# One more attention job of the output projection from split parts, with fewer constant products and moved subtractions

## The chip, the cores and the metric

The kernel runs on one core of a Trainium2 chip. The metric is the device time of one execution in microseconds (us). The kernel before takes 1575.31 us, the median of 3 runs (1574.83 to 1578.89).

## The reference, cut to what matters

The program computes two decoder layers over 256 positions of width 2048. What the change touches lies in the first layer's mixer and in the second layer's:

```python
def even_layer(x, ...):                      # layer 0
    proj = rms_norm(x, norm_w) @ w_in        # q, k, v, indexer parts, GLU input
    attn = dsa_attention(...)                # 8 heads x 128 = 1024 channels
    conv = conformer_conv(glu_in, ...)       # GLU -> causal depthwise conv, 31 taps,
                                             # 1024 channels -> LayerNorm over channels -> silu
    return x + jnp.concatenate([attn, conv], axis=-1) @ w_out

def odd_layer(x, norm_w, pool_w, pool_scale):  # layer 1
    # d = windowed mean of rms_norm(x) minus itself, 4 groups of 512 channels
    mixed = jnp.einsum('bsgc,gce->bsge', d, pool_w)
    return x + pool_scale * mixed
# each layer is followed by a mixture of experts (hier_moe)
```

LayerNorm needs the mean and the variance over the 1024 channels, so the convolution must be complete before either is known, and nothing of `conv @ w_out` can begin before the variance.

## The kernel before, in words

All 256 positions stand on chip. Weights come in blocks of 1 MB (128 partitions x 2048 numbers) into a ring of 8 slots. A block is used in one of two ways.

*Split stream.* Each half block (a unit, 128 x 1024) is rounded by ScalarE into `split_hi` (line 688, type fp32r), then VectorE writes the rest, block minus high part, into `split_lo` (line 1092). TensorE makes three products of each pair of tiles, high x high, high x low and low x high (`product`, lines 1785 to 1787). There are SPLITS = 4 buffers of each: ScalarE may write unit u only when TensorE has used unit u-4 (`mixer_used`). `split_past(name, n)` on ScalarE or VectorE means: have all units up to n past the end of job `name` in the stream.

*Direct.* `direct_job` (line 1866) multiplies the fp32 block as it lies in the ring by fp32 data. No splitting is done for it. Each such product shows as two records on TensorE.

The output projection of layer 0 has 8 jobs: `wa0` to `wa3` (attention half of the input, output columns by 512) and `wc0` to `wc3` (convolution half). Before, `wa0`, `wa1`, `wa2` are direct and `wa3` and all `wc` come from the stream. A streamed job has 4 units of 12 products (`out_job`), and a function `beside_...(q)` puts other work ahead of its unit q. The order on TensorE is written out by hand: `wa0`, `wa1`, `wa2`, `wa3`, `wc0` to `wc3`. Beside `wa2` stand the two halves of the channel sum for the mean (`channel_sum`, line 1933, the second half waits for all 248 steps of the convolution); beside `wa3` the sums of squares for the variance (`squares_sum`, line 1944, ahead of unit 0) and the spreading of the row scales (`rstd`, line 2019, ahead of unit 2).

The convolution is done on VectorE, one instruction for each tap and chunk (`convolve(n)`: the next n of 248 instructions, line 1137), in order with everything else that VectorE does. Around the change VectorE's order is: 20 and 31 taps, the low part of the attention output (`attn_parts[1]`, line 1092), the addition of `wa0` to x (`add_job`, line 1329), the remaining taps, two units of `wa3`, scaling of the mean (1343), subtraction of it (1347), two units of `wa3`, addition of `wa1`, variance (1351), diagonal of row scales (1354), addition of `wa2`, two units of `wc0`, then `scale_conv(j)` (1362), `silu(j)` (1368) and `lo_of_conv(j)` (1092), which alternate with ScalarE (870, 874, 688). `wc0` waits for `lo_of_conv(0)`.

At the very start TensorE multiplies a tile of ones (`keep_busy_small(24)`, 8 and 8, line 1736) between transpositions of x, whose results nobody reads.

In the second layer's mixer, `pool_split(u)` (VectorE part at line 1096) writes the low part of unit u of the pooling weights, scaled by the norm weights. VectorE's order there is: last additions of the experts, `sum_squares(2)` (1088), scaling of the band matrices (1697), then 8 low parts of the pooled input `dT` with `pool_split` 1, 2 and 3 behind the first, third and fifth. TensorE's first product waits for the eighth low part and for units 0 and 1.

SyncE issues the weight loads in ring order and waits for a slot to be free: for a direct block until TensorE used it, for a streamed block until VectorE wrote its low part.

Of the kernel before, what the change touches and what calls it, by code (L numbers as in the profile page):

```python
# [102 lines left out]


STREAM = [(name, 8) for name in ("ag0", "ag1", "kvi", "iq0", "iq1", "q0", "q1", "ag2", "ag3")]
STREAM += [(name, 4) for name in ("wa3", "wc0", "wc1", "wc2", "wc3")]
DIRECT = [f"wa{n}" for n in range(3)]

STREAM_END = {name: sum(k for _, k in STREAM[:i + 1]) for i, (name, _) in enumerate(STREAM)}

# [1 line left out]
def job_number(name):  # L112

    return sum(n not in STREAM_END and n not in DIRECT for n, _ in JOBS[:JOB_AT[name] + 1])

# [15 lines left out]
def build(nc, a):  # L131
    x_in, out = a["x"], a["out"]
    ctx = ExitStack()
    with ctx:
# [102 lines left out]
        def cat_cut(at, a, b):  # L237

            return [cat[:, at + i * a * b:at + (i + 1) * a * b].rearrange("p (a b) -> p a b", b=b) for i in range(2)]
# [3 lines left out]
        attnT = xn[:, NT * HEADS * HD:].rearrange("p (h s) -> p h s", h=HEADS)  # L243
        attn_parts = cat_cut(2 * D, HEADS, SEQ)
# [224 lines left out]

        DIRECT_BLOCKS = range(DIRECT0, DIRECT0 + 2 * len(DIRECT))  # L470

# [36 lines left out]
        def wait_for_job(eng, name):  # L508

            if name in STREAM_END:  # L510
                eng.wait_ge(mixer_used, STREAM_END[name])
            elif name in DIRECT:
                eng.wait_ge(direct_used, 2 * DIRECT.index(name) + 2)
            else:
# [171 lines left out]
        def _(act):  # L686
# [35 lines left out]
            def split_past(name, more):  # L722

                split_to(STREAM_END[name] + more)
# [130 lines left out]
            copy(attn_parts[0], attnT).then_inc(attn_hi, 1)  # L855
            split_past("ag3", 4)
            for h in range(2):
                act.wait_ge(ln_step, 2 + h)
                half = slice(4 * h, 4 * h + 4)
                nc.scalar.activation(vsq[:, half, :], conv[:, half, :], ACT.Square).then_inc(squared, 1)  # L860
# [209 lines left out]
        def _(dve):  # L1070
# [14 lines left out]
            def sum_squares(i):  # L1085

                dve.wait_ge(sq_done, 8 * (i + 1))
                nc.vector.tensor_reduce(sumsq[:, i, :], part_sq[:, i], X, ALU.add).then_inc(sum_done, 1)
# [15 lines left out]
            def wait_job(name):  # L1104
                wait_for_job(dve, name)
# [20 lines left out]
            def convolve(more):  # L1126

                end = min(at[1] + more, taps_open[0])
                for n in range(at[1], end):
                    c, w = conv_ops[n]  # L1130
                    tap = cw_sb[:, w * CC + c:w * CC + c + 1]
                    if w == 0:
                        ts(conv[:, c, :], uT[:, c, 0:SEQ], tap, vec_sb[:, V_CB + c:V_CB + c + 1], ALU.mult, ALU.add) \
                            .then_inc(conv_step, 1)
                    else:
                        dve.wait_ge(conv_step, n - 1)
                        stt(out=conv[:, c, :], in0=uT[:, c, w:w + SEQ], scalar=tap, in1=conv[:, c, :],  # L1137
                            op0=ALU.mult, op1=ALU.add).then_inc(conv_step, 1)
                at[1] = end

            def split_to(end, taps=0):

                for u in range(at[0], end):
                    b, n = split_block(u), 2 * (KVW + IKW) if u // 2 in kvi_at else HALF
                    dve.wait_ge(mixer_hi, u + 1)
                    low(split_lo[:, u % SPLITS, 0:n], raw_half(b % RING, u % 2, n), split_hi[:, u % SPLITS, 0:n]) \
                        .then_inc(mixer_lo, 1)
                    convolve(taps)
                at[0] = end

            def split_past(name, more, taps=0):
                split_to(STREAM_END[name] + more, taps)
# [75 lines left out]
            n = 0  # L1228
# [18 lines left out]
            n = 0  # L1247
# [83 lines left out]
            def add_job(name):  # L1331
                wait_job(name)
                for t, bank in enumerate(BANKS[name]):
                    add_x(int(name[-1]), t, bank)

            convolve(31)
            dve.wait_ge(attn_hi, 1)
            low(attn_parts[1], attnT, attn_parts[0]).then_inc(attn_lo, 1)
            add_job("wa0")
            convolve(CONV_TAPS)  # L1340
            split_past("ag3", 2)
            wait_job("mean")
            ts(mean_sb, ps[:, BANKS["mean"][0], 0:SEQ], 1.0 / CCH, None, ALU.mult).then_inc(ln_step, 1)
            dve.wait_ge(ln_step, 1)
            for h in range(2):
                half = conv[:, 4 * h:4 * h + 4, :]
                tt(half, half, mean_sb.unsqueeze(1).to_broadcast([P, 4, SEQ]), ALU.subtract).then_inc(ln_step, 1)
            split_past("ag3", 4)
            add_job("wa1")
            wait_job("var")  # L1350
            ts(rvar, ps[:, BANKS["var"][0], 0:NT], 1.0 / CCH, EPS, ALU.mult, ALU.add).then_inc(ln_step, 1)
# [330 lines left out]
            def pool_split(u):  # L1682
                dve.wait_ge(pool_hi, u + 1)
                for k in range(2):
                    cols = slice(k * 512, (k + 1) * 512)
                    last = low_of(split_lo[:, u % SPLITS, cols], raw_half((POOL0 + u // 2) % RING, u % 2)[:, cols],
                                  vec_sb[:, V_PN + 2 * u + k:V_PN + 2 * u + k + 1], split_hi[:, u % SPLITS, cols])
                last.then_inc(pool_lo, 1)

            moe_dve(0)  # L1690

            sum_squares(2)
            dve.wait_ge(band_in, 16)
            dve.wait_ge(rstd_done, 3)
# [3 lines left out]
            for i in range(8):  # L1698
                dve.wait_ge(pooled_hi, i + 1)
                low(dT[1][:, 2 * i:2 * i + 2, :], ps[:, i, :].rearrange("p (c s) -> p c s", c=2), dT[0][:, 2 * i:2 * i + 2, :]) \  # L1700
                    .then_inc(dT_out, 1)
                if i in (0, 2, 4):
                    pool_split(1 + i // 2)
            for i in range(8):
                g, t = i // 2, i % 2
                if i == 0:
# [20 lines left out]
        def _(pe):  # L1727
# [5 lines left out]
            def keep_busy_small(n):  # L1733

                for i in range(n):
                    mm(ps[:, 0, 0:P], ones[:], ones[:], start=True, stop=True)  # L1736

            pe.wait_ge(set_up, 1)
            keep_busy_small(24)
            pe.wait_ge(ident_in, 16)  # L1740

            def turn_vectors():
# [100 lines left out]
            def out_job(name, parts, between=lambda q: None):  # L1843

                start_job(name)
                for q in range(4):
                    between(q)
                    w = next_unit(2, 512)
                    for k in range(2):
                        for t, b in enumerate(BANKS[name]):  # L1850
                            last = product(ps[:, b, :], pick_parts(parts, ALL, 2 * q + k, slice(t * P, (t + 1) * P)),
                                           pick_parts(w, ALL, k), q == 0 and k == 0, q == 3 and k == 1)
                    last.then_inc(mixer_used, 1)

            def direct_job(name, src, between=lambda q: None):

                start_job(name)
                for q in range(4):
                    between(q)
                    b = DIRECT0 + 2 * int(name[-1]) + q // 2  # L1860
                    if q % 2 == 0:
                        pe.wait_ge(mixer_in[b % RING], mixer_landed(b))
                    w = raw_half(b % RING, q % 2).rearrange("p (k n) -> p k n", k=2)
                    for k in range(2):
                        for t, bank in enumerate(BANKS[name]):
                            last = mm(ps[:, bank, :], src[:, 2 * q + k, t * P:(t + 1) * P], w[:, k, :],  # L1866
                                      start=q == 0 and k == 0, stop=q == 3 and k == 1)
                    if q % 2:
                        last.then_inc(direct_used, 1)
# [132 lines left out]
            def beside_wa2(q):  # L2002
                if q == 0:
                    pe.wait_ge(conv_step, CONV_TAPS // 2)
                    channel_sum("mean", conv, 0)
                if q == 2:
                    pe.wait_ge(conv_step, CONV_TAPS)
                    channel_sum("mean", conv, 1)

            def beside_wa3(q):  # L2010
                if q == 0:
                    for h in range(2):
                        pe.wait_ge(squared, h + 1)
                        squares_sum(h)
                if q == 2:
                    start_job("rstd")
                    pe.wait_ge(diag_done, NT)
                    for t in range(NT):
                        last = mm(ps[:, BANKS["rstd"][0], t * P:(t + 1) * P], ones[:], rstd_diag[:, t, :], start=True, stop=True)
                    last.then_inc(job_done, 1)  # L2020
# [3 lines left out]
            for j in range(4):  # L2024
                turn_first(j)
                if j % 2:
                    keep_busy_small(8)
            channels_job("ag0", beside_ag0)
            channels_job("ag1", beside_ag1)
            pe.wait_ge(row_scale_out, 1)  # L2030
# [11 lines left out]
            pe.wait_ge(oT_out, 4)  # L2042
            direct_job("wa0", attnT)
            direct_job("wa1", attnT)
            direct_job("wa2", attnT, beside_wa2)
            pe.wait_ge(attn_lo, 1)
            out_job("wa3", attn_parts, beside_wa3)

            def beside_wc(n, q):
# [217 lines left out]
```

## Time and profile before

| | |
|---|---|
| profiled execution | 1575.78 us, of which the span of instructions is 1573.9 us |
| TensorE (PE) busy | 1539.9 us, 98% |
| VectorE (DVE) busy | 1393.9 us, 89% |
| ScalarE (ACT) busy | 1082.8 us, 69% |
| chain that ended last | PE 86%, DVE 11%, ACT 2% |
| DMA | 471.62 MB, mean 300 GB/s |

TensorE is nearly always busy, so the table alone does not tell what bounds a stage. The slices of the page show the first mixer (to about 380 us) as the place where TensorE and VectorE are both near full while DMA falls to 84 to 177 GB/s; the two expert stages run TensorE full with DMA at 340 to 380 GB/s. The chain gives VectorE a share of 11%, nearly all of it in the first mixer.

### The profile page before, as it was taken

How to read it: one execution, taken by the hardware profiler on the slowest of the kernel's cores; microseconds unless marked ns; L12 is line 12 of the kernel's file. 1: busy time of each engine (PE TensorE's matmuls, PEld its weight loads, DVE VectorE, ACT ScalarE, POOL GpSimd, SP SyncE). 2: the span in 40 equal slices, each digit the busy share in tenths (PEclk: the TensorE clock that was granted, in tenths of full speed). 3: DMA queues.
4: the chain of work that ended last, by engine and by line, in shares of the span. 5: the costliest groups of instructions: out<-in, count | busy, mean ns of one | idle time of the engine just before them, and what ended most of it. 6: DMA issues, size and time to landing. Idle time of an engine off the chain costs nothing.

```text
span 1573.9 us, 21864 instructions
## 1 busy us (share of the span) xinstructions
PE 1539.9 (98%) x7520; PEld 1269.2 (81%) x7520; DVE 1393.9 (89%) x1698; ACT 1082.8 (69%) x1287; POOL 12.8 (1%) x23
## 2 busy tenths in 40 slices
PE   9999999999999999999999999999999999999998
PEld 8998795677788878878887877778888887888886
DVE  4898989766999999999999987699999999999997
ACT  5444352164878777877877785587877887787785
POOL 0000100000000000000000000000000000000000
PEclk9999999999999999999999999999999999999999
DMA  8974442543999999999999993299999999999993
GB/s 230 362 249 140 151 144 84 177 154 122 342 370 377 362 362 370 368 345 375 382 350 359 376 359 105 83 339 386 375 348 379 376 362 345 370 375 349 369 371 142
DMA packets 159756, 471.62 MB, mean 300 GB/s; under 512 B 20922, under 2 KB 40844, under 8 KB 159284
## 3 DMA queue, kind: packets, MB, share of 16 engines
q1 hardware_dynamic: 158148, 466.85, 80.8%
q10 hardware_dynamic: 1520, 3.63, 0.6%
q8 instruction: 51, 0.84, 0.2%
q14 instruction: 37, 0.30, 0.0%
HBM read 468.34 MB, written 4.21 MB: 300 GB/s over the span
## 4 chain that ended last, share of the span: by engine, by line
PE 86%; DVE 11%; ACT 2%; issue 1%; POOL 0%; DVEq 0%
PE ps L1785 26%; PE ps L1787 26%; PE ps L1786 26%; DVE work L1137 3%; DVE split_lo L1092 3%; PE ps L1731 2%; PE ps L2104 2%; PE ps L2090 1%; PE ps L1766 1%; DVE cat L1092 1%; PE ps L1736 1%; ACT split_hi L688 1%; PE ps L1886 0%; PE ps L1866 0%; DVE work L1258 0%
## 5 line engine op out<-in xcount | busy, mean ns | idle before, releaser
L688 ACT ACTIVATE split_hi<-ring 128x1024 fp32r<-128x1024 f32 x860 | 904.6, 1058 | 298.2 <-PE ps L1787 286.1
L1092 DVE TENSOR_TENSOR split_lo<-ring,split_hi 128x1024 fp32r<-128x1024 f32 x860 | 1026.4, 1218 | 93.0 <-ACT split_hi L688 58.3
L1785 PE MATMUL ps<-split_hi,cat 128*128 128x512 f32 (+1 forms) x1744 | 687.1, 394 | 11.7 <-DVE split_lo L1092 5.4
L1787 PE MATMUL ps<-split_hi,cat 128*128 128x512 f32 (+1 forms) x1744 | 677.8, 389 | 0.0
L1786 PE MATMUL ps<-split_lo,cat 128*128 128x512 f32 (+1 forms) x1744 | 677.5, 388 | 0.0
L1785 PEld LDWEIGHTS ps<-split_hi,cat 128*128 128x128 f32 x1744 | 328.2, 188 | 93.8 <-issue 15.6
L1787 PEld LDWEIGHTS ps<-split_hi,cat 128*128 128x128 f32 x1744 | 327.6, 188 | 68.5
L1786 PEld LDWEIGHTS ps<-split_lo,cat 128*128 128x128 f32 x1744 | 328.1, 188 | 63.6
L1785 PE MATMUL ps<-cat,split_hi 128*128 128x256 f32 x384 | 111.5, 290 | 7.4 <-DVE split_lo L1092 7.4
L1787 PE MATMUL ps<-cat,split_lo 128*128 128x256 f32 x384 | 110.1, 287 | 0.0
L1786 PE MATMUL ps<-cat,split_hi 128*128 128x256 f32 x384 | 110.0, 287 | 0.0
L1137 DVE SCALAR_TENSOR_TENSOR work<-work,cw_sb 128x256 f32<-128x256 f32 x240 | 99.4, 475 | 0.0
L1785 PEld LDWEIGHTS ps<-cat,split_hi 128*128 128x128 f32 x384 | 75.1, 196 | 9.4 <-DVE split_lo L1092 4.7
L1787 PEld LDWEIGHTS ps<-cat,split_lo 128*128 128x128 f32 x384 | 75.1, 196 | 0.0
L1786 PEld LDWEIGHTS ps<-cat,split_hi 128*128 128x128 f32 x384 | 75.0, 195 | 0.1
L1092 DVE TENSOR_TENSOR cat<-ps,cat 128x512 fp32r<-128x512 f32 (+1 forms) x56 | 46.4, 835 | 2.1 <-ACT cat L688 1.9
L688 ACT ACTIVATE cat<-ps 128x512 fp32r<-128x512 f32 (+1 forms) x56 | 38.9, 706 | 10.0 <-PE ps L2199 6.0
L1565 DVE TENSOR_TENSOR x_sb<-ps,x_sb 128x1024 f32<-128x1024 f32 x32 | 38.8, 1216 | 4.8 <-PE ps L2104 4.8
L1866 PE MATMUL ps<-ring,xn 128*128 128x512 f32 x96 | 41.8, 593 | 0.7 <-ACT xn L688 0.7
L2104 PE MATMUL ps<-cat,pickT 128*128 128x512 f32 x128 | 33.8, 391 | 3.1 <-DVE cat L1092 3.1
L1866 PEld LDWEIGHTS ps<-ring,xn 128*128 128x128 f32 x96 | 18.2, 190 | 23.1 <-issue 21.5
L2104 PEld LDWEIGHTS ps<-cat,pickT 128*128 128x128 f32 x128 | 23.9, 188 | 8.8 <-DVE cat L1092 3.9
(200 smaller groups left out, 686.3 us busy)
## 6 DMA issues: line engine op xcount, KB each, us to landing
ring<-in_w_gate SPq DMA_DIRECT2D x128, 1024.0 KB, 6.1
ring<-in_w_up SPq DMA_DIRECT2D x128, 1024.0 KB, 6.3
ring<-in_w_down SPq DMA_DIRECT2D x128, 1024.0 KB, 6.1
ring<-in_w_in_e SPq DMA_DIRECT2D x16, 1024.0 KB, 7.1
ring<-in_w_out_e SPq DMA_DIRECT2D x16, 1024.0 KB, 5.1
ring<-in_w_in_e SPq DMA_DIRECT2D x30, 512.0 KB, 4.6
ring<-in_pool_w_o SPq DMA_DIRECT2D x4, 1024.0 KB, 5.7
ring<-in_w_in_e SPq DMA_DIRECT2D x12, 256.0 KB, 6.1
```

The source lines that it names most:

```text
L688: return nc.scalar.activation(out, in_, ACT.Copy, scale=scale)
L1092: return tt(dst, full, hi.bitcast(F32), ALU.subtract)
L1137: stt(out=conv[:, c, :], in0=uT[:, c, w:w + SEQ], scalar=tap, in1=conv[:, c, :], op0=ALU.mult, op1=ALU.add).then_inc(conv_step, 1)
L1565: tt(cols, ps[:, bank:bank + 2, :].rearrange("p b n -> p (b n)"), cols, ALU.add).then_inc(m["x_moved"], 1)
L1731: return nc.tensor.transpose(dst, src, ident[0:n, 0:n])
L1736: mm(ps[:, 0, 0:P], ones[:], ones[:], start=True, stop=True)
L1766: last = mm(ps[0:20, LOGIT_BANKS[l][0], 0:SEQ], router_w[:, l, c, :], hT32[:, c, :], start=c == 0, stop=c == KC - 1)
L1785: mm(out, sh, mh, start=start, stop=False, **how)
L1786: mm(out, sh, ml, start=False, stop=False, **how)
L1787: return mm(out, sl, mh, start=False, stop=stop, **how)
L1866: last = mm(ps[:, bank, :], src[:, 2 * q + k, t * P:(t + 1) * P], w[:, k, :], start=q == 0 and k == 0, stop=q == 3 and k == 1)
L2104: last = mm(ps[:, bank, :], pickT[:, t, :], y[part][:, b * 512:(b + 1) * 512], start=part == 0, stop=part == 1)
```

## The change

`wa2` leaves the direct jobs and joins the stream ahead of `wa3`; the channel sums, sums of squares and row scales move from `wa2`/`wa3` to later places; VectorE takes the four units of `wa2` and one unit of `wa3` between convolution steps and adds `wa0` ahead of the attention's low part; the products of ones fall from 24 to 17 and from 8 to 3 twice; `pool_split(1)` moves ahead of `sum_squares(2)`, and units 2 and 3 behind the first and fourth low part.

```diff
-STREAM += [(name, 4) for name in ("wa3", "wc0", "wc1", "wc2", "wc3")]
-DIRECT = [f"wa{n}" for n in range(3)]
+STREAM += [(name, 4) for name in ("wa2", "wa3", "wc0", "wc1", "wc2", "wc3")]
+DIRECT = [f"wa{n}" for n in range(2)]
...
@@ ScalarE
             split_past("ag3", 4)
             for h in range(2):
+                split_past("ag3", 6 + h)
                 act.wait_ge(ln_step, 2 + h)
...
@@ VectorE
             convolve(31)
+            add_job("wa0")
             dve.wait_ge(attn_hi, 1)
             low(attn_parts[1], attnT, attn_parts[0]).then_inc(attn_lo, 1)
-            add_job("wa0")
+            split_past("ag3", 4)
+            convolve(20)
+            split_past("wa2", 1)
             convolve(CONV_TAPS)
-            split_past("ag3", 2)
             wait_job("mean")
...
-            split_past("ag3", 4)
+            split_past("wa2", 4)
             add_job("wa1")
...
+            pool_split(1)
             sum_squares(2)
...
-                if i in (0, 2, 4):
-                    pool_split(1 + i // 2)
+                if i in (0, 3):
+                    pool_split(2 + i // 3)
...
@@ TensorE
-            keep_busy_small(24)
+            keep_busy_small(17)
...
                 if q == 0:
                     pe.wait_ge(conv_step, CONV_TAPS // 2)
                     channel_sum("mean", conv, 0)
-                if q == 2:
+            def beside_wa3(q):
+                if q == 0:
                     pe.wait_ge(conv_step, CONV_TAPS)
                     channel_sum("mean", conv, 1)
-
-            def beside_wa3(q):
-                if q == 0:
+                if q == 2:
                     for h in range(2):
                         pe.wait_ge(squared, h + 1)
                         squares_sum(h)
-                if q == 2:
+                if q == 3:
                     start_job("rstd")
...
                 if j % 2:
-                    keep_busy_small(8)
+                    keep_busy_small(3)
...
             direct_job("wa1", attnT)
-            direct_job("wa2", attnT, beside_wa2)
             pe.wait_ge(attn_lo, 1)
+            out_job("wa2", attn_parts, beside_wa2)
             out_job("wa3", attn_parts, beside_wa3)
```

## Rows read from the trace of the kernel before

**Rows 1.** Timeline of VectorE, 269 to 312 us: start, length, instructions, idle before.
```profile
269.86 19.47 DVE L1137 SCALAR_TENSOR_TENSOR work<-work,cw_sb 128x256 f32<-128x256 f32 x49
289.25 2.35 DVE L1092 TENSOR_TENSOR split_lo<-ring,split_hi 128x1024 fp32r<-128x1024 f32 x2
291.52 0.41 DVE L1343 TENSOR_SCALAR work<-ps 128x256 f32<-128x256 f32 x1
291.97 2.36 DVE L1347 TENSOR_TENSOR work<-work 128x1024 f32<-128x1024 f32 x2
...
301.75 0.16 DVE L1351 TENSOR_SCALAR work<-ps 128x2 f32<-128x2 f32 x1 [3.95 <-PE ps L1944]
302.72 0.48 DVE L1354 TENSOR_SCALAR work<-const_sb,work 128x128 f32<-128x128 f32 x2 [0.81 <-POOL work L678]
303.12 1.28 DVE L1329 TENSOR_TENSOR x_sb<-ps,x_sb 128x512 f32<-128x512 f32 x2
...
310.00 1.23 DVE L1092 TENSOR_TENSOR split_lo<-ring,split_hi 128x1024 fp32r<-128x1024 f32 x1 [1.44 <-ACT split_hi L688]
311.15 1.28 DVE L1362 TENSOR_TENSOR work<-work,ps 128x512 f32<-128x512 f32 x2
```

**Rows 2.** Timeline of TensorE, 252 to 317 us.
```profile
252.47 27.73 PE L1866 MATMUL ps<-ring,xn 128*128 128x512 f32 x64 [0.69 <-ACT xn L688]
280.04 1.89 PE L1933 MATMUL ps<-work,ones 128*128 128x256 f32 x8
281.76 7.03 PE L1866 MATMUL ps<-ring,xn 128*128 128x512 f32 x16
289.39 1.99 PE L1933 MATMUL ps<-work,ones 128*128 128x256 f32 x8 [0.59 <-DVE work L1137]
...
298.08 3.63 PE L1944 MATMUL ps<-ones,work 128*128 128x1 f32 x32
...
305.98 0.39 PE L1785 MATMUL ps<-split_hi,cat 128*128 128x512 f32 x1
...
308.71 0.61 PE L2019 MATMUL ps<-work,ones 128*128 128x128 f32 x4
...
316.85 0.47 PE L1785 MATMUL ps<-split_hi,cat 128*128 128x512 f32 x1 [2.07 <-DVE cat L1092]
```

**Rows 3.** Timeline of ScalarE, one unit of the stream.
```profile
308.91 1.06 ACT L688 ACTIVATE split_hi<-ring 128x1024 fp32r<-128x1024 f32 x1 [1.61 <-PE ps L1787]
```

**Rows 4.** Stretches: PE, PEld, DVE, ACT, POOL busy, then granted clock, DMA.
```profile
301.60:305.30 3.70, 3.70 (x12) 2.89 (x12) 1.84 (x5) 0.00 (x0) 0.69 (x1) 0.56 1.05 402
...
314.80:316.85 2.05, 0.00 (x0) 0.03 (x1) 1.69 (x4) 2.05 (x4) 0.00 (x0) 1.00 0.28 114
```

**Rows 5.** Stretches, TensorE alone: busy, granted clock, DMA share, GB/s.
```profile
179.80:182.00 2.20, 0.18 (x1) 1.00 0.19 62
...
183.00:186.00 3.00, 3.00 (x16) 0.50 0.28 55
...
959.40:962.40 3.00, 0.00 (x1) 1.00 0.31 66
```

**Rows 6.** Timeline of the start on TensorE: products of ones, then unit 2.
```profile
1.08 7.52 PE L1736 MATMUL ps<-ones 128*128 128x128 f32 x48 [1.08 <-DVE ones L1076]
...
9.62 1.95 PE L1736 MATMUL ps<-ones 128*128 128x128 f32 x16
...
20.61 0.36 PE L1785 MATMUL ps<-cat,split_hi 128*128 128x256 f32 x1
```

**Rows 7.** Timeline of ScalarE at the start: unit 2 of the stream.
```profile
17.83 1.06 ACT L688 ACTIVATE split_hi<-ring 128x1024 fp32r<-128x1024 f32 x1 [4.19 <-DMA ring<-in_w_in_e]
```

**Rows 8.** Timeline of VectorE in the second mixer.
```profile
949.34 0.16 DVE L1088 TENSOR_REDUCE sumsq<-part_sq 128x2 f32<-128x8 f32 x1 [1.49 <-ACT xn L698]
...
954.12 1.41 DVE L1096 SCALAR_TENSOR_TENSOR split_lo<-ring,vec_sb,split_hi 128x512 fp32r<-128x512 f32 x2
...
960.48 1.88 DVE L1092 TENSOR_TENSOR cat<-ps,cat 128x512 fp32r<-128x512 f32 x3
```

## The prediction

> **What bounds the kernel now.** The page was read first, for the shares: TensorE is busy 98% of the span, which says little, since a busy TensorE in the first mixer can be one that merely fills the time until VectorE is ready. So the next view was the timeline of VectorE and TensorE side by side over the output projection. The reader should see two things. VectorE runs without a gap up to the last tap at 289.25 us [rows 1], and TensorE waits for exactly that tap: its second channel sum begins at 289.39 after 0.59 us of idle time put down to VectorE's line 1137 [rows 2]. So up to that point VectorE sets the time, TensorE is nearly level with it, and any work added to VectorE ahead of the last tap comes out in full. Behind the tap the bound changes: VectorE idles 3.95 us for the sums of squares [rows 1], TensorE is full until 314.8, and then idles 2.07 us for the low part of the first convolution chunk, which starts `wc0` at 316.85 [rows 2, 4]. From `wc0` on TensorE carries the chain (the additions, transpositions and expert stages follow it), so the start of `wc0` is what the change in this stage must be judged by. The expert stages are untouched; I take it that a shift arrives at the end in full, since TensorE waits there for no load.
>
> **The output projection, step by step.** A direct job is 32 records; 64 of them take 27.57 us (252.47 to 280.04), so one job is 13.8 us. Three-part products follow each other by 0.2275 us (12 between 305.98 and 308.71, one unit, 2.73 us), so a streamed job is 10.9 us [rows 2]. TensorE loses 2.9 us of work. In exchange VectorE gets four more subtractions and ScalarE four more copies.
>
> VectorE, ahead of the last tap. The attention's low part and the addition of `wa0` swap places; `wa0` is done at about 266.4, when VectorE comes, so both still end at 269.86. Then:
> - four units of `wa2`: a pair takes 2.27 us until the next starts (289.25 to 291.52), so 4.54 us, to 274.40. Their copies on ScalarE were made long before, in an idle stretch.
> - 20 taps at 0.396 us (49 between 269.86 and 289.25) [rows 1]: 7.91 us, to 282.31.
> - one unit of `wa3`. Its copy needs the buffer of `wa2`'s unit 0, which TensorE frees only when it has finished `wa1` (280.04), the first channel sum (to 281.76) and the 12 products (to 284.49) [rows 2], and drained them (0.2 us: the last product of the unit before 308.71 frees ScalarE at 308.91) [rows 3]. The copy lets VectorE start 1.09 us later (308.91 to 310.00) [rows 1, 3]: 285.78. **VectorE stands still for 3.5 us with the taps queued behind this wait**, and all of the LayerNorm behind the taps. This is the step that decides.
> - the subtraction, 1.14 us, and 29 taps, 11.48 us: the last tap ends at 298.40, against 289.25. That is 9.15 us later, of which 4.5 are the new units, 1.1 the advanced one and 3.5 the wait.
>
> TensorE meanwhile finishes `wa2` at 281.76 + 10.92 = 292.7 and has nothing until 298.4, since the second channel sum now stands ahead of `wa3`: 5.7 us idle.
>
> Behind the last tap, first at the full clock. Second channel sum from 298.54, and VectorE reads the mean at 300.6 (289.39 to 291.38 is 1.99, plus 0.1); scaling and both subtractions as in [rows 1], to 303.36. Then unit 1 of `wa3` to 304.5; TensorE did unit 0 by 303.0, waits, and does unit 1 to 307.3. The squares of ScalarE are ready by 305.4, so the sums of squares run 307.3 to 310.8 (3.49 us, the length it had) [rows 2]. From the start of those sums VectorE reads the variance 3.67 us later, the diagonals end 1.37 us after that (301.75 to 303.12) [rows 1]: 312.3. Next on VectorE stand the addition of `wa2` (1.2 us) and two units of `wc0` (2.3 us; before, the second of them was waited for until 310.00 anyway): 315.8. The row scales are spread by then even if TensorE's unit 2 runs at half rate. The first `scale_conv` starts at 315.8 against 311.15, and `wc0` 5.70 us later as before (311.15 to 316.85) [rows 1, 2]: 321.5. **So this stage costs +4.6 us with no clock lost.** TensorE's 2.9 us come back only as shorter waits. The bounds are +1.2 (if the 3.5 us wait should not be, by an earlier release that I don't see) and +8 with all clock losses below.
>
> **The clock.** After 2.0 us of idle time (180.0 to 182.0) TensorE worked at a granted clock of 0.50, that is 1.2 GHz, from 183 to 186 [rows 5]; after the tiny one-column sums of squares it had 0.56 over 301.6 to 305.3 [rows 4]. After 2.05 us of idle time from 314.8 and 3.0 us from 959.4 it kept 1.00 [rows 4, 5]. So a gap of two or three us may or may not do it; 5.7 us is far longer than the gap that did. I take it that the second channel sum runs at half rate: 1.7 us more, all of it on the chain, as VectorE, ScalarE and the sums of squares wait for it. `wa3` unit 0 behind it has 1.5 us of room. Bounds 0 and +2.7 (that unit too). TensorE then ends `wa3` at about 320 and waits some 3 us for `wc0` where it waited 2.07: `wc0` may start at 1.2 GHz too. Its second and third unit waited for VectorE before, which absorbs about half: between 0 and +0.8, with 0.5 taken.
>
> The Trainium skill (TensorE: Matmul & The Clock Gate, "Why this matters for your kernels") warns against idle gaps between bursts of matmuls, because the clock falls back to half rate after one. It speaks against this change at the 5.7 us gap: by it the stage costs +6.3, by the rows of 314.8 and 962.4 taken alone +4.6. The trace so far sides with it for the gap at 180 and not for the other two.
>
> **The start.** 17 instead of 24 products of ones remove 14 records at about 0.112 us (16 in 1.8) [rows 6], 1.6 us, since those removed are full-rate ones at the end; twice 10 records more remove 2.2 us. The first unit would begin 3 us earlier, at 11.0, ready data or not: the first x and gains are landed, and the first subtraction is done at about 10.9. But unit 2 needs a block whose copy starts at 17.83, held by DMA [rows 7]; its low part is ready 1.09 + 1.15 later, at 20.1, and its products begin at 20.61 today [rows 6]. So of 3.8 us removed 0.45 arrive, and TensorE idles 2.4 us ahead of unit 2. If that gap takes the clock down, unit 2 costs 1.7 more: bounds -0.45 and +1.25, and -0.4 taken, since gaps of 2.05 and 3.0 us left the clock up in [rows 4, 5]. Behind it TensorE is full to 100 us.
>
> **The second mixer.** VectorE is the chain from 953.5 to 962.36: eight low parts of 0.6 and three `pool_split` of 1.32 (954.12 to 955.44), the last low part ending where TensorE starts [rows 8]. `pool_split(1)` moves to 947.8, into the 1.49 us that VectorE idles before `sum_squares` at 949.34; 1.32 us fit, and its high part is done at 941. The eighth pooled tile is copied at 960.04, so the eighth low part can end at 961.0: **-1.3 us**. Bounds -1.5 and 0 (if `sum_squares` is pushed by as much). The new order of units 2 and 3 leaves them done by 958.6, ahead of group 1's need.
>
> SyncE's queue: the slots of `wa2` are now freed by its low parts, 14 us earlier, those of `wa3` a few us later. The blocks behind them (`wc2`, `wc3`) are used after 340, so nothing waits.
>
> **Sum**, against the profiled execution of 1575.78 (span 1573.9 plus 1.9 around it): +4.6 +1.7 +0.5 -0.4 -1.3 = +5.1, which gives 1580.9; that execution lies 0.5 above the median of 1575.31, so the forecast for a median is 1580.4, put at 1580.5. What a measurement of this kernel can tell from no change is 0.3%, 4.7 us: the forecast lies just beyond it.
>
> **Rivals.**
> - *The same chain, clock kept.* +4.6 -0.4 -1.3 = +2.9: 1578.3. For it: the two gaps without a fall. Against: neither was much over 3 us, and this one is 5.7.
> - *TensorE is the bound throughout.* Then the 2.9 us of the shorter job arrive, with 1.3 and 0.4: -4.6, 1570.7. It decides if VectorE's taps have slack of 9 us against TensorE. Against it stands the 0.59 us wait at 289.39 in [rows 2]: they have none. This is the case on the other side.
> - *No wait ahead of the advanced unit.* The stage costs +1.2, and the total is -0.5: 1574.8. For it: only that ScalarE is idle there. Against: the buffer is TensorE's to free.
> - *Clock lost at the start and at `wc0` in full.* +5.1 +1.7 +0.5: 1582.6.
>
> **How the numbers follow.** Forecast 0.55, clock kept 0.20, no wait 0.09, all clocks lost 0.08, TensorE bound 0.08. The forecast's own spread is 1578.5 to 1582.5, and about 0.39 of its 0.55 lies over +0.3%. Slower: 0.39 + 0.08 = 0.47. Faster: 0.06 of the TensorE case. Same: the rest, 0.16 + 0.20 + 0.09 + 0.02 = 0.47. The range leaves out the TensorE case and most of the case without a wait: 1576 to 1583.5.
>
> **What would show it.** The last tap near 298 instead of 289, with VectorE idle 3 us or more ahead of one subtraction, released by ScalarE's copy; TensorE idle over 5 us ahead of its second channel sum, and a granted clock near 0.5 there; `wc0` starting 6 us later; the second mixer's first product 1.3 us earlier relative to `sum_squares`; the start's unit 2 held by DMA at 17.8. I am wrong if VectorE does not idle ahead of that unit, or if TensorE waits for the taps by less than 2 us.

## The result, and the profile after

The changed kernel takes 1582.96 us, the median of 9 runs (1580.93 to 1585.17), against 1577.47 us for the kernel before (9 runs in all). The ratio is 1.0036, with a 95% interval of 1.0028 to 1.0045: slower by about 5.7 us. The forecast was +5.1 us, and 1580.5 us for the median. The profiled execution took 1582.92 us with a span of 1581.0, so 7.1 us more span than the one before. Single executions spread by several us, for a reason shown further down, so the account below is made of stretches of the traces, and what is faster or slower is told by the ratios.

The timeline of VectorE over the output projection, after (start, length, instructions, idle before), answers to [rows 1]:

```profile
269.27 4.62 DVE L1093 TENSOR_TENSOR split_lo<-ring,split_hi 128x1024 fp32r<-128x1024 f32 x4
273.82 8.00 DVE L1138 SCALAR_TENSOR_TENSOR work<-work,cw_sb 128x256 f32<-128x256 f32 x20
285.26 1.23 DVE L1093 TENSOR_TENSOR split_lo<-ring,split_hi 128x1024 fp32r<-128x1024 f32 x1 [3.45 <-ACT split_hi L688]
286.40 11.57 DVE L1138 SCALAR_TENSOR_TENSOR work<-work,cw_sb 128x256 f32<-128x256 f32 x29
301.92 0.42 DVE L1346 TENSOR_SCALAR work<-ps 128x256 f32<-128x256 f32 x1 [3.94 <-PE ps L1937]
...
312.45 0.16 DVE L1354 TENSOR_SCALAR work<-ps 128x2 f32<-128x2 f32 x1 [2.45 <-PE ps L1948]
...
315.02 2.35 DVE L1093 TENSOR_TENSOR split_lo<-ring,split_hi 128x1024 fp32r<-128x1024 f32 x2
317.34 1.29 DVE L1365 TENSOR_TENSOR work<-work,ps 128x512 f32<-128x512 f32 x2
```

The reader should see the third line: one subtraction of 1.2 us, preceded by 3.45 us of standing still, with 29 taps behind it. The last tap ends near 298, 9 us later than in [rows 1]. ScalarE's copy, for which it waited, could begin when TensorE had freed the buffer, and not before. The timeline of ScalarE:

```profile
284.17 1.06 ACT L688 ACTIVATE split_hi<-ring 128x1024 fp32r<-128x1024 f32 x1 [26.66 <-PE ps L1791]
```

ScalarE was idle for 26.66 us ahead of it, so it is a matter of the buffer and not of a busy engine. The timeline of TensorE, which answers to [rows 2]:

```profile
251.83 27.73 PE L1870 MATMUL ps<-ring,xn 128*128 128x512 f32 x64 [0.69 <-ACT xn L688]
279.40 1.89 PE L1937 MATMUL ps<-work,ones 128*128 128x256 f32 x8
...
298.12 3.75 PE L1937 MATMUL ps<-work,ones 128*128 128x256 f32 x8 [5.89 <-DVE work L1138]
...
308.78 3.63 PE L1948 MATMUL ps<-ones,work 128*128 128x1 f32 x32
...
323.05 0.73 PE L1789 MATMUL ps<-split_hi,cat 128*128 128x512 f32 x1 [3.01 <-DVE cat L1093]
```

The second channel sum waits 5.89 us for the last tap and then takes 3.75 us where it took 1.99. The stretches of TensorE (busy, granted clock, DMA share, GB/s) say why, and answer to [rows 5]:

```profile
292.30:298.10 5.80, 0.00 (x0) 0.80 0.00 0
298.10:302.30 4.20, 4.17 (x10) 0.50 0.00 0
302.70:305.00 2.30, 2.30 (x11) 1.00 0.00 0
312.90:316.20 3.30, 3.30 (x10) 0.50 0.11 39
323.10:326.40 3.30, 3.30 (x8) 0.50 0.00 0
```

The granted clock stood at 0.50 when the sum began, that is 1.2 GHz; it had fallen during the idle stretch ahead of it (0.80 on average over 292.30 to 298.10). The products behind the sums of squares ran at 1.2 GHz as before, and so did most of the first unit of `wc0` behind its gap of 3.01 us.

The second mixer, timeline of VectorE, answers to [rows 8]:

```profile
955.38 1.41 DVE L1097 SCALAR_TENSOR_TENSOR split_lo<-ring,vec_sb,split_hi 128x512 fp32r<-128x512 f32 x2
956.96 0.16 DVE L1089 TENSOR_REDUCE sumsq<-part_sq 128x2 f32<-128x8 f32 x1 [0.17 <-ACT xn L698]
...
966.19 2.48 DVE L1093 TENSOR_TENSOR cat<-ps,cat 128x512 fp32r<-128x512 f32 x4
```

`pool_split(1)` lies in the idle time ahead of `sum_squares`, which is not pushed: it still waits 0.17 us for ScalarE.

With the span cut at the same instructions in both traces (the difference of two starts, us):

| stretch | before | after | change |
|---|---|---|---|
| start to the first direct product | 252.47 | 251.83 | -0.6 |
| to the first product of `wc0` | 64.38 | 71.22 | +6.8 |
| to the sorting of tokens (first product of split x) | 64.49 | 65.47 | +1.0 |
| first experts, to the first pooled copy | 571.54 | 571.99 | +0.5 |
| second mixer, to the second sorting | 51.32 | 50.22 | -1.1 |
| second experts, to the end | 569.70 | 570.27 | +0.6 |

### The profile page after: what moved, and what is told of

It is laid out like the page before. It is cut to its first block, busy times and chain, and to the rows that moved or that the text cites. A ratio compares the mean times of both kernels' runs of the same rounds, so it can differ in the third digit from the quotient of the medians.

```text
span 1581.0 us, 21838 instructions
## 1 busy us (share of the span) xinstructions
PE 1537.9 (97%) x7502; PEld 1271.6 (80%) x7502; DVE 1398.8 (88%) x1702; ACT 1087.0 (69%) x1291; POOL 12.1 (1%) x23
## 4 chain that ended last, share of the span: by engine, by line
PE 86%; DVE 9%; ACT 2%; issue 2%; DMA 1%; SPq 0%; DVEq 0%; POOL 0%; ACTq 0%
PE ps L1789 26%; PE ps L1791 25%; PE ps L1790 25%; DVE split_lo L1093 3%; PE ps L1735 2%; PE ps L1870 2%; PE ps L2107 2%; DVE work L1138 2%; PE ps L2093 1%; PE ps L1770 1%; ACT split_hi L688 1%; DVE cat L1093 1%; DMA ring<-in_w_in_e 1%; PE ps L1890 0%; DVE work L1259 0%
## 5 line engine op out<-in xcount | busy, mean ns | idle before, releaser
L1789 PE MATMUL ps<-split_hi,cat 128*128 128x512 f32 (+1 forms) x1760 | 694.8, 395 | 13.0 <-DVE split_lo L1093 7.2
L1791 PE MATMUL ps<-split_hi,cat 128*128 128x512 f32 (+1 forms) x1760 | 684.6, 389 | 0.0
L1790 PE MATMUL ps<-split_lo,cat 128*128 128x512 f32 (+1 forms) x1760 | 684.5, 389 | 0.0
L1789 PEld LDWEIGHTS ps<-split_hi,cat 128*128 128x128 f32 x1760 | 331.8, 189 | 95.7 <-issue 15.3
L1791 PEld LDWEIGHTS ps<-split_hi,cat 128*128 128x128 f32 x1760 | 331.3, 188 | 69.2
L1790 PEld LDWEIGHTS ps<-split_lo,cat 128*128 128x128 f32 x1760 | 331.7, 188 | 64.6
L698 ACT ACTIVATE xn<-x_sb 128x512 f32<-128x512 f32 x32 | 19.8, 624 | 16.1 <-DVE x_sb L1330 9.7
L1735 PEld LDWEIGHTS ps<-const_sb,work 128*128 128x128 f32 (+3 forms) x164 | 24.8, 190 | 5.4 <-ACT work L688 1.9
```

Source lines behind the costliest of these rows:

```text
L698: nc.scalar.activation(xn[:, t * D + b * 512:t * D + (b + 1) * 512], x_sb[:, t, b * 512:(b + 1) * 512], ACT.Square, accum_out=part_sq[:, i ...
L1735: return nc.tensor.transpose(dst, src, ident[0:n, 0:n])
L1789: mm(out, sh, mh, start=start, stop=False, **how)
L1790: mm(out, sh, ml, start=False, stop=False, **how)
L1791: return mm(out, sl, mh, start=False, stop=stop, **how)
```

## The experiments

Each kernel's ratio is to the kernel before, which ran beside it: the first four share 29 runs of it (median 1577.91 us), the last four another 35 (median 1577.18 us). The changed kernel's ratio of 1.0036 is to the nine of the result. So medians are compared only within a group of four, and ratios across them.

**The output projection's edits alone** (start and pool order put back):

```diff
-            keep_busy_small(17)
+            keep_busy_small(24)
-                    keep_busy_small(3)
+                    keep_busy_small(8)
-            pool_split(1)
             sum_squares(2)
...
-                if i in (0, 3):
-                    pool_split(2 + i // 3)
+                if i in (0, 2, 4):
+                    pool_split(1 + i // 2)
```

> The changed kernel with its start (24, 8 and 8 products of ones) and its pool_split order put back: the output projection's edits alone. Theory (VectorE holds the stage, TensorE loses its clock in the gap): the whole loss is here and the two other edits gave back 1.3 and 0.4 to 0.65 us, so +7.0 to +7.9 us over the kernel before, ratio 1.0045 to 1.005. Rival (the start or the second mixer costs something that shows later): no more than the changed kernel's +5.7, ratio 1.0036 or under.

Measured 1589.11 us (6 runs), ratio 1.0061 (1.0044 to 1.0078). The sign of the theory holds, the two other edits do give time back, but they give back more than I said: the excess over the changed kernel is some 4 us in the ratios and 6.6 in the spans. The cuts of the trace put 4.1 us of it in the second mixer (54.35 against 50.22). Of the rest, 1.0 us lies ahead of the first direct product and 1.1 us behind the start of `wc0`, where the clock stayed down for longer than in the changed kernel. In the second mixer TensorE waits 3.11 us, and this time the clock fell. The stretches of both places, columns as above:

```profile
324.24:330.03 5.79, 5.79 (x14) 0.50 0.00 0
...
969.50:972.60 3.10, 0.00 (x1) 0.86 0.35 69
972.60:976.00 3.40, 3.39 (x8) 0.50 0.68 277
976.00:980.00 4.00, 4.00 (x13) 0.68 0.00 0
```

The same gap left the clock at 1.00 in [rows 5]. So moving `pool_split(1)` is worth 1.1 to 1.3 us by the traces, and another 1.6 (in the trace of the start alone, below) to 3 us (here) in executions in which the gap takes the clock down. The higher ratio is thus in part the clock's doing and not only that of the two edits put back.

**The wait without the work**: 30 taps instead of 20 ahead of the advanced unit, all work the same.

```diff
-            convolve(20)
+            convolve(30)
             split_past("wa2", 1)
```

> The changed kernel with 30 instead of 20 taps ahead of the advanced unit of wa3. Nothing else moves: VectorE does the same work, but reaches the subtraction at about 285.7 us, when ScalarE's copy is done. Theory: the 3.45 us of waiting are lost time, so the last tap ends 3.4 us earlier, TensorE's gap shrinks from 5.9 to about 2.5 us, and the time falls by 3.4 us, by up to 5.1 if the clock then stays up (ratio to before 1.0005 to 1.0015). Rival (TensorE or the chain behind the taps has room that absorbs the wait): time unchanged, ratio 1.0036.

Measured 1580.02 us (12 runs), ratio 1.0010 (1.0001 to 1.0020). VectorE, timeline:

```profile
286.36 1.23 DVE L1093 TENSOR_TENSOR split_lo<-ring,split_hi 128x1024 fp32r<-128x1024 f32 x1
287.50 7.61 DVE L1138 SCALAR_TENSOR_TENSOR work<-work,cw_sb 128x256 f32<-128x256 f32 x19
```

No idle time stands at the end of the first line: the subtraction no longer waits. TensorE's second channel sum, timeline:

```profile
295.25 2.87 PE L1937 MATMUL ps<-work,ones 128*128 128x256 f32 x8 [2.39 <-DVE work L1138]
```

The stretch to `wc0` is 66.82 us, 4.4 less than in the changed kernel, and the ratios differ by 0.0026, 4.1 us. The 4.4 us are the 3.45 of the wait and 0.9 of the clock, as the sum took 2.87 us behind the shorter gap and not 3.75. The wait was lost time; nothing behind the taps absorbed it.

**The unit behind the last tap**:

```diff
-            split_past("wa2", 1)
             convolve(CONV_TAPS)
+            split_past("wa2", 1)
```

> The changed kernel with the advanced unit of wa3 taken behind the last tap. Theory: last tap 4.6 us earlier (3.45 wait, 1.14 subtraction); the subtraction then lies beside the second channel sum; TensorE's gap is 1.3 us, too short for a fall of the clock. Time falls by 4.6 us, with the clock by 6.3: ratio to before 0.9995 to 1.0007. Rival: unchanged at 1.0036, or the unit is late for TensorE's first products of wa3 and 1.1 us come back.

Measured 1578.32 us (12 runs), ratio 1.0000 (0.9990 to 1.0010); the stretch to `wc0` is 64.74 us, 6.5 less. TensorE, timeline:

```profile
292.92 1.97 PE L1937 MATMUL ps<-work,ones 128*128 128x256 f32 x8 [1.25 <-DVE work L1138]
...
316.03 0.77 PE L1789 MATMUL ps<-split_hi,cat 128*128 128x512 f32 x1 [4.54 <-DVE cat L1093]
```

The gap is 1.25 us, and the sum is back at 1.97. The place of one subtraction makes up the whole difference between the changed kernel and a ratio of 1. That ratio still holds the gains of the start and the pool order, so it does not mean that the streamed job is free (see the last two experiments). TensorE's shorter job is worth nothing here: it comes back as 4.54 us of waiting for VectorE ahead of `wc0`.

**TensorE kept at work in its gaps**, VectorE's order untouched:

```diff
                 if q == 0:
+                    keep_busy(13, 3)
                     pe.wait_ge(conv_step, CONV_TAPS)
...
+            keep_busy(6, 3)
             out_job("wc0", convT, ...)
```

> The changed kernel with 13 products of constants (128x256) on TensorE ahead of the wait for the last tap and 6 ahead of wc0, into a bank that nobody uses then. VectorE's order is untouched. Theory: of the loss, 1.7 us are the second channel sum at half rate and 0.8 the first unit of wc0 at half rate; with TensorE kept at work the granted clock stays at 1.00 and the time falls by 2 to 2.5 us, ratio to before 1.002 to 1.0025. Rival (the half rate is covered by other waits): unchanged, ratio 1.0036; or the products run into the sum and add 0.5 us.

Measured 1581.50 us (12 runs), ratio 1.0019 (1.0008 to 1.0031). TensorE, timeline and then stretches:

```profile
298.73 2.00 PE L1937 MATMUL ps<-work,ones 128*128 128x256 f32 x8 [0.18 <-DVE work L1138]
...
321.86 0.47 PE L1789 MATMUL ps<-split_hi,cat 128*128 128x512 f32 x1 [1.94 <-DVE cat L1093]
```
```profile
293.00:299.00 6.00, 5.82 (x27) 1.00 0.00 0
...
321.86:326.00 4.14, 4.14 (x12) 0.64 0.00 0
```

The sum takes 2.00 us, the stretch to `wc0` 69.30, 1.9 less than in the changed kernel; the ratios differ by 0.0017, 2.7 us, with intervals that overlap a little. The sum still waits for the same tap, so the 1.9 us of the stretch are the clock's share at the sum: with products running in the gap it kept 1.00. At `wc0` six products were too few: 1.94 us of waiting were left and the clock fell again.

**The start alone** (24, 8, 8 to 17, 3, 3 on the kernel before):

> The kernel before with 17, 3 and 3 products of ones instead of 24, 8 and 8, nothing else. Theory: TensorE reaches unit 2 of the first job early and waits for the DMA of its block, so of 3.8 us removed 0.4 to 1.2 arrive (the changed kernel gained 0.64 at its attention projection), and where the clock falls in that gap nothing or a loss of 1 us: ratio 0.9992 to 1.0005. Rival (the start is bound by TensorE): 3.8 us arrive, ratio 0.9976.

Measured 1576.11 us (11 runs), ratio 0.9999 (0.9988 to 1.0010). TensorE waits for the low part of unit 2, as before but longer (timeline):

```profile
19.47 0.35 PE L1785 MATMUL ps<-cat,split_hi 128*128 128x256 f32 x1 [1.14 <-DVE split_lo L1092]
```

In this execution unit 2 began 1.1 us earlier than in [rows 6], 0.25 us of which were left at the attention's projection. The full 3.8 us are excluded; whether anything arrives the ratio does not tell. Ahead of `wc0` the clock fell in this trace behind a gap of 2.06 us, which the kernel before had passed at 1.00 [rows 4].

**The pool order alone** (on the kernel before):

> The kernel before with the pool_split order of the changed one, nothing else. Theory: the first product of the second mixer starts 1.3 us earlier relative to the first pooled copy, ratio 0.9992. Where the kernel before lets TensorE's clock fall in its gap of 3.1 us there (as the stage-alone kernel did, at a cost of 3 us), the shorter gap of 1.8 us saves those as well: ratio down to 0.9975. Rival (VectorE's early pool_split pushes sum_squares): no gain, ratio 1.000.

Measured 1576.09 us (11 runs), ratio 0.9996 (0.9988 to 1.0005). Against the rival, the second mixer is 50.01 us instead of 51.32, 1.3 us less; the ratio alone does not tell that from nothing.

**Both on the kernel before**, `wa2` direct:

> The kernel before with the start and the pool_split order of the changed one, wa2 still direct. Theory: the two gains add, 1.7 to 2.5 us: ratio 0.9985 to 0.9990, below both kernels. Rival (gains only exist on top of the streamed wa2): ratio 1.000.

Measured 1573.07 us (12 runs), ratio 0.9978 (0.9969 to 0.9988): the fastest of all, below both kernels, and more than expected. Its profiled execution is not typical (1576.11 us): there TensorE waited longer ahead of the last transpositions of the attention's output, and the clock fell.

```profile
246.25 1.88 PE L1732 MATMUL ps<-const_sb,xn 128*128 128x128 f32 x8 [2.90 <-ACT xn L688]
```

These 8 transpositions took 1.15 us in the changed kernel behind a gap of 1.42. The pair gains more than the two alone (0.0022 against 0.0005, apart by about their intervals), and a good part of that goes with the clock. The mean granted clock over an execution was 0.9968 on average for the pair, 0.9955 for the pool order alone, 0.9949 for the start alone and 0.9953 for the kernel before. An estimate: work done at 1.2 GHz takes twice as long, so an execution with a mean clock of c loses at most (1 - c) of its time by it, and 0.0013 more clock over 1575 us is worth up to 2 us of the 3.0 between the medians of the pool order alone and of the pair. The one execution of the pool order alone with 0.997 took 1573.50 us, like the pair's. One part is in the trace of the start alone, where the clock fell in the second mixer's gap of 3 us (granted 0.50 over 961.7 to 965.0) and took 1.6 us back; the pair has no such gap. Why the pool order alone so seldom reached 0.997 stays open.

The pair is also the measure for the streamed job itself. The changed kernel differs from it by the output projection's edits alone, and the ratios by 0.0058, some 9 us.

**The unit behind the last tap, and 10 products of constants ahead of `wc0`**:

> The kernel with the advanced unit behind the last tap, plus 10 products of constants ahead of wc0, where TensorE waited 4.5 us and then ran at 1.2 GHz. Theory: the clock stays at 1.00 and wc0's first unit runs at full rate: 0.8 to 1.7 us less than without, ratio to before 0.9988 to 0.9995. Rival (wc0 waits for VectorE anyway): no change, ratio 1.000.

Measured 1576.95 us (12 runs), ratio 1.0004 (0.9996 to 1.0013). TensorE's stretch at the start of `wc0`:

```profile
318.10:325.00 6.90, 6.90 (x32) 1.00 0.00 0
```

The clock stayed, and the way from the first direct product to the first transposition of x is 79.6 us against 80.8 without the products, 86.6 in the changed kernel and 78.7 in the kernel before. The ratio shows no gain over the unfilled one: inconclusive in time, and even with no clock lost at the sum and at `wc0` the streamed job is not ahead of the direct one in this stage. Against the pair, which has the same start and pool order and `wa2` direct, it is 3.9 us slower (1576.95 against 1573.07, with the same runs of the kernel before beside both). The traces place 1.6 us of it between the first direct product and the sorting and 0.9 in the two expert stages; the profiled executions don't show the rest, and the mean granted clock is lower (0.9950 against 0.9968).

## Why the prediction was right

*VectorE sets the time up to the last tap.* Right. Idle time ahead of the advanced unit: forecast 3.5, measured 3.45. The second experiment removed it alone and the time fell by 4.1 us.

*Four new subtractions come out in full.* Right: 4.55 us (269.27 to 273.82) against 4.54.

*TensorE's 2.9 us are worth nothing.* Right: the waits ahead of the second channel sum and of `wc0` grew from 0.59 and 2.07 us to 5.89 and 3.01, and in the third experiment, with the first of them down to 1.25, the second was 4.54.

*The stage costs +4.6 us at full clock.* The changed kernel's stretch to `wc0` grew by 6.8, and 1.9 of it went with the filled gap: 4.9 are left. Forecast and trace agree along the way: last tap 9.15 us later against 9.4, counted from the first direct product.

*The channel sum at 1.2 GHz, +1.7.* Right: 3.75 against 1.99 us, and 1.9 by the fourth experiment. This was the step with the weakest ground, since two of three gaps in the rows had kept their clock; the runs later showed both outcomes for gaps of 2 to 3 us, and a fall in both traces with a gap of 5.89. The Trainium skill's advice against idle gaps between bursts (TensorE: Matmul & The Clock Gate, "Why this matters for your kernels") agreed with this trace: 0.50 behind the gap of 5.89 us.

*Half of a clock loss at `wc0`, +0.5.* Mis-sized: the fall came, and the next stretch is 1.0 us longer.

*The second mixer, -1.3.* Measured -1.1 in the pair of profiles and -1.3 with the edit alone. Its second effect, the clock kept in executions that would lose it, was not foreseen.

*The start, -0.4.* -0.64 at the first direct product, and -0.25 with the edit alone. That the number fits is luck: unit 2's block landed 1.2 us earlier (its copy starts at 16.65 instead of 17.83), so that the gap was 0.92 us and not 2.4, and unit 2 began 1.5 us earlier and not 0.45. The first direct product starts at 251.3 to 252.6 us in six of the seven traces with the short start (254.86 in the pair's) and at 252.47, 252.80 and 254.12 in the three with the long one, so a term of this size is not shown by one pair of traces.

*What was missing.* Each expert stage is longer by 0.5 us, in all six traces with the streamed job (570.12 to 570.27 for the second) and in none of the four with the direct one (569.70 to 569.77). I had taken these stages as untouched. In the changed kernel one subtraction of one pass is late in each stage; the first:

```profile
842.26 0.50 PE L1789 MATMUL ps<-split_hi,cat 128*128 128x512 f32 x1 [0.98 <-DVE split_lo L1093]
```

The same wait is 0.58 us in the kernel before, and the one of the second stage (1187.61) is 0.94 against 0.58. In the first, VectorE's instruction ahead of these subtractions (line 1593) waited 0.60 us for TensorE in place of 0.20, and the DMA view has a packet of instructions (queue 14) there in the changed kernel (836 to 843) and none in the kernel before (829 to 836). That such a load delays VectorE is not tested, so the cause stays open; the instructions of these stages are the same in both kernels. So the sum, +5.1 against +7.1 in the pair of profiles and some 5.7 by the ratio, was short by this 1.0, by 0.5 in the stage up to `wc0` and by 0.5 behind it; the error is of terms, the mechanism held.

*The time itself.* The median of 1582.96 us lies 2.5 us above the forecast, and only about half a us of that is the change's. The rest is the start of the count: the kernel before has a median of 1577.47 over 9 runs, 2.2 above the 1575.31 of the first 3.

## What to carry to other kernels

Where one engine sets the pace, an instruction put into its queue early is dear when its input depends on another engine's release: here one subtraction of 1.1 us, ten taps too early, cost 3.5 us of standing still, and the gap that this left on TensorE cost up to 1.8 us more by its clock. Making a job shorter on an engine that then waits is no gain, and the longer gap can make that engine slower, as it did here. Look for the engine that idles last ahead of the stage's end before moving work from one to another: the two small edits (fewer products of ones at the start, and a subtraction moved into VectorE's idle time) were the only part of this change that paid, at a ratio of 0.9978 together; alone neither was told from nothing.

## What the runs showed of the hardware that I had not expected

Gaps of TensorE of the same length do or do not take its clock down. In the second mixer a gap of 3.10 us left it at 1.00 in the kernel before, and 3.11 us took it to 0.50 in two other traces, the output projection's edits alone and the start alone, at a cost of 3.0 and 1.6 us. Ahead of the attention 2.90 us were followed by a fall in one trace, 1.42 us were not in another. Ahead of `wc0`, 2.07 us were not in the kernel before [rows 4], 2.06 us were in the start alone, and 1.94 us in the fourth experiment.

That this differs from one execution to the next of one kernel is seen in the times, as only one execution of each kernel has a trace. The kernel before ran 64 times beside the experiments, within 1574.58 to 1582.84 us. The 6 executions with a mean granted clock of 0.993 took 1582.2 us on average, the 25 with 0.996 took 1575.9, the 3 with 0.997 took 1575.3. The spread of these times is thus for the most part the clock's: by the estimate above, 0.004 of clock over 1575 us are 6.3 us.

The pool order seems to narrow the spread as well: its 11 runs lie within 3.5 us, and 10 of the pair's 12 below 1574.2, while the 11 of the start alone lie within 6.5.
